# Splitting the first latent projections of a hybrid diffusion step into two halves, the lower one between two pairs of modulation chunks

## What is computed

```python
m_ctx = jnp.split(jax.nn.silu(c_ctx) @ mod_w[l] + mod_b[l], 6, axis=-1)      # shift, scale, gate, ...
m_lat = jnp.split((jax.nn.silu(c) @ mod_w[l] + mod_b[l])[:, None, :], 6, axis=-1)
hp = _modulate(xp, m_ctx[0], m_ctx[1])                                       # x * (1 + scale) + shift
hs = _modulate(xs, m_lat[0], m_lat[1])
q_a, f_f, f_b, i_a, g_a, cq, ckv_raw, kr = jnp.split(h @ w_in, AB_SPLITS, axis=-1)
q = (_rms_norm(cq_raw, q_norm_g) @ w_uq)
kv = (_rms_norm(ckv_raw, kv_norm_g) @ w_ukv)
```

## Time and profile before

| | before |
|---|---|
| median of 3 runs, us | 1290.81 |
| the profiled execution: its own time, us | 1289.75 |
| its span, us | 1287.9 |
| mean granted TensorE clock, share of full | 0.978 |
| PE busy | 1188.9 us (92%) |
| DVE busy | 597.9 us (46%) |
| ACT busy | 352.0 us (27%) |
| instructions | 17510 |
| chain that ended last, by engine | PE 78%, DVE 6%, DMA 6% |
| DMA, mean over the span | 209 GB/s |

### The profile page before, as it was taken

The page is one execution under the profiler, slowest core; times in us unless marked ns, Lnnn a source line. Parts: engine busy times, 40 slices in busy tenths (PEclk is TensorE's granted clock), DMA queues, the critical chain, the costliest instruction groups (busy, mean ns, idle before and its releaser), DMA issues.

```text
span 1287.9 us, 17510 instructions
## 1 busy us (share of the span) xinstructions
PE 1188.9 (92%) x6755; PEld 680.1 (53%) x6755; DVE 597.9 (46%) x1173; ACT 352.0 (27%) x695; POOL 186.9 (15%) x177
## 2 busy tenths in 40 slices
PE   5999999999999989999999877999999998999774
PEld 2554555545546577456555435755555555555441
DVE  2223333310136666768432217079986865332218
ACT  1333444421214543212122125311023111221122
POOL 1000000010000001131323120800000332222210
PEclk9999999999999999998999898999999998999988
DMA  9504476773211204826799969021114438999973
GB/s 348 210 25 177 142 254 239 289 270 114 89 33 40 74 10 163 340 83 232 299 407 409 406 244 393 23 91 66 66 66 171 156 128 316 392 410 408 354 293 150
DMA packets 99666, 269.79 MB, mean 209 GB/s; under 512 B 12811, under 2 KB 15154, under 8 KB 98690
## 3 DMA queue, kind: packets, MB, share of 16 engines
q1 hardware_dynamic: 83632, 234.55, 48.3%
q0 software_dynamic: 15632, 34.02, 7.1%
q10 hardware_dynamic: 322, 0.12, 0.0%
HBM read 257.68 MB, written 31.93 MB: 225 GB/s over the span
## 4 chain that ended last, share of the span: by engine, by line
PE 78%; DVE 6%; DMA 6%; SPq 4%; ACT 3%; issue 2%; ACTq 0%; POOLq 0%; DVEq 0%
PE ps L2285 18%; PE ps L2296 14%; PE ps L2797 8%; PE ps L2814 4%; PE ps L2175 4%; PE ps L2437 3%; DMA ln_rows<-in_moe_w_up 3%; PE ps L2600 3%; PE ps L2785 2%; PE ps L2581 2%; PE ps L2404 2%; PE ps L2746 2%; SPq L710 1%; PE ps L2699 1%; SPq L707 1%
## 5 line engine op out<-in xcount | busy, mean ns | idle before, releaser
L2285 PE MATMUL ps<-h_cm,weights 128*128 128x512 f32 (+1 forms) x832 | 226.8, 434 | 0.0
L2285 PEld LDWEIGHTS ps<-h_cm,weights 128*128 128x128 f32 x832 | 126.3, 191 | 104.0 <-issue 103.7
L2296 PE MATMUL ps<-weights,mix_cm 128*128 128x512 f32 x256 | 112.2, 595 | 0.0
L1769 DVE SCALAR_TENSOR_TENSOR scratch<-scratch,taps_cm 128x655 f32<-128x655 f32 x120 | 101.5, 897 | 2.5 <-ACT scratch L1325 1.0
L2296 PEld LDWEIGHTS ps<-weights,mix_cm 128*128 128x128 f32 x256 | 47.9, 190 | 56.5 <-issue 56.4
L2067 DVE TENSOR_TENSOR scratch<-ps,scratch 128x128 f32<-128x128 f32 x38 | 11.1, 292 | 143.1 <-ACT scratch L1373 143.1
L2296 PE MATMUL ps<-weights,h_cm 128*128 128x512 f32 (+1 forms) x208 | 71.4, 502 | 0.0
L2797 PE MATMUL ps<-weights,scratch 128*64 128x256 f32 x384 | 68.3, 389 | 1.8 <-DMA weights<-in_moe_w_up 1.8
L1442 DVE COPY mod_parts<-ps 128x512 f32<-128x512 f32 x24 | 16.6, 691 | 93.3 <-PE ps L2175 93.3
L1697 DVE SCALAR_TENSOR_TENSOR mix_cm<-mix_cm,gate_rows,ps 128x128 f32<-128x128 f32 x152 | 46.0, 345 | 25.1 <-PE ps L2545 23.0
L2296 PEld LDWEIGHTS ps<-weights,h_cm 128*128 128x128 f32 x208 | 36.3, 190 | 35.6 <-issue 35.6
(11 more groups left out here) (449 smaller groups left out, 2133.1 us busy)
## 6 DMA issues: line engine op xcount, KB each, us to landing
weights<-in_mod_w SPq DMA_DIRECT2D x13, 2048.0 KB, 8.9
x_tm<-in_mod_w SPq DMA_DIRECT2D x10, 2048.0 KB, 8.6
weights<-in_moe_w_gate SPq DMA_DIRECT2D x24, 512.0 KB, 11.6
weights<-in_moe_w_up SPq DMA_DIRECT2D x24, 512.0 KB, 13.4
weights<-in_moe_w_down SPq DMA_DIRECT2D x24, 512.0 KB, 15.7
scratch<-in_moe_w_down SPq DMA_DIRECT2D x21, 512.0 KB, 12.9
weights<-in_ab_w_in SPq DMA_DIRECT2D x5, 2048.0 KB, 12.8
weights<-in_cd_w_in SPq DMA_DIRECT2D x5, 2048.0 KB, 16.0
```

Of the source, the lines that this page charges most:

```text
L1769: ins = V.scalar_tensor_tensor(out=CO[:, j, 0:655], in0=UP[:, j, k:k + 655], scalar=CW[:, 4 * k + j:4 * k + j + 1], in1=CO[:, j, 0:655], o ...
L2285: ins = T.matmul(ps(*name)[:, a:b], w[:, k, col:col + 128], HT[:, k, a:b], start=(k == 0), stop=(k == KD - 1))
L2296: ins = T.matmul(ps(*name)[:, at:at + w.shape[2]], src[:, k, t * 128:t * 128 + 128], w[:, k, :], start=(k == 0), stop=(k == KD - 1))
```

## The change

The lower half of the features (512 of 1024) needs only chunks 0 and 2. The change loads these two first and forms, for all five tiles, the half of the latents that comes from the lower features (groups `ca`), with chunks 1 and 3 and their products in between. ACT puts these partial sums into `CQ`. Afterwards the upper half is formed (groups `cq`), and DVE adds it to `CQ`, which is an added instruction of 672 columns for each tile. The transposes of x are split the same way: `xa` for blocks 0 to 3, `xT` for 4 to 7, each with its slot. The columns of c get a group of their own, `c`, ahead of `vec`. Two times seven short products on the constants are issued whose results nobody reads (`warm_up`). The lower part of the 160 wide weights gets its own place in `mix_cm`. Chunk 3 goes to slot 0, which chunk 0 leaves. GpSimd's four loads of norm vectors and cache wait for the lower latent weights.

```diff
-FIRST_MODS = [("mod", 0), ("mod", 1), ("modb", 0), ("mod", 2), ("modb", 1), ("mod", 3), ("modb", 2), ("modb", 3)]
+FRONT = [("c",), ("mod", 0, 0), ("vec",), ("modb", 0, 0), ("mod", 0, 2), ("modb", 0, 2), ("xa", 0), ("xa", 1), ("ca", 0), ("xa", 2), ("ca", 1),
+         ("xa", 3), ("ca", 2), ("mod", 0, 1), ("modb", 0, 1), ("ca", 3), ("mod", 0, 3), ("modb", 0, 3), ("xa", 4), ("xT", 0, 0), ("ca", 4)]
...
             for t in range(NT):
+                if t + 1 < NT:
+                    g.append(("xT", 0, t + 1))
                 g.append(("cq", t))
...
-        for c in range(4):
-            mod_item(0, c, c)
+        for c, at in ((0, 0), (2, 2), (1, 3), (3, 0)):
+            mod_item(0, c, at)
...
-        proj_item(("cqb",), 2, ("cq", 4), w_in, 3072, AB_IN)
+        cqb_to, cqb_from = slot3(2)[:, 0:8 * (AB_IN - 3072)].rearrange("p (k n) -> p k n", k=8), col_chunk(w_in, 3072, AB_IN)
+        item(("cqb",), 2, ("cq", 4), [(cqb_to[:, 4:8, :], cqb_from[:, 4:8, :])])
+        cqb_low = OTF[:, 4096:4096 + 4 * (AB_IN - 3072)].rearrange("p (k n) -> p k n", k=4)
...
+                    if items[n] == ("mod", 0, 1):
+                        sp.dma_start(X[:, 0:2, :], xs[:, 0:2, :]).then_inc(d_x[0], 16)
+                        sp.wait_ge(d_first, 16)
                         sp.dma_start(cqa_to[:, 0:4, :], cqa_from[:, 0:4, :]).then_inc(d_first, 16)
+                        sp.dma_start(cqb_low, cqb_from[:, 0:4, :]).then_inc(d_first, 16)
+                        sp.dma_start(X[:, 2:4, :], xs[:, 2:4, :]).then_inc(d_x[1], 16)
...
-            pool.wait_ge(d_first, 32)
+            pool.wait_ge(d_first, 48)
...
-            act.wait_ge(d_vec_a, 16 * 11)
+            act.wait_ge(d_c, 32)
             A_(V1[0:16, :], V1[0:16, :], ACT.Silu).then_inc(c_silu, 1)
...
             h_evac0(0)
-            h_evac0(1)
             for t in range(NT):
-                filled(act, "cq", t)
-                release(A_(CQ[:, t, :], ps("cq", t)[:, 0:672], ACT.Copy), "cq", t)
+                if t + 1 < NT:
+                    h_evac0(t + 1)
+                first_half(t)
+            for t in range(NT):
                 emptied(act, "cq", t)
...
             for t in range(NT):
+                if t + 1 < NT:
+                    h_evac0(t + 1)
+                filled(dve, "cq", t)
+                release(V.tensor_tensor(CQ[:, t, :], ps("cq", t)[:, 0:672], CQ[:, t, :], ALU.add), "cq", t)
...
+            def warm_up(at, count):
+
+                for _ in range(count):
+                    T.matmul(at, ident, C[:, 0:128], start=True, stop=True)
...
+                if (l, c) == (0, 0):
+                    warm_up(ps("mod", 0, 0)[:, 512:640], 7)
...
+            def latents(name, t, ks):
+
+                open_group(pe, *name)
+                for at, w in ((0, wa), (512, wb if ks[0] else cqb_low)):
+                    for k in ks:
+                        ins = T.matmul(ps(*name)[:, at:at + w.shape[2]], HT[:, k, t * 128:t * 128 + 128], w[:, k, :],
+                                       start=(k == ks[0]), stop=(k == ks[-1]))
+                close_group(ins, *name)
...
             for t in range(NT):
-                if t:
-                    emptied(pe, "xT", 0, t)
-                    pe.wait_ge(h_half, t + 1)
-                    project_tm(("cq", t), HT, t, [(0, wa), (512, wb)])
-                if t + 2 < NT:
-                    x_turn0(t + 2)
+                if t + 1 < NT:
+                    x_turn0(("xT", 0, t + 1), t + 1)
+                emptied(pe, "xT", 0, t)
+                latents(("cq", t), t, range(4, KD))
                 turn_normed(t - 1 if t else NT)
```

More of the change, by code:

```diff
@@ L160, in psum_groups @@
 def psum_groups():
-    g = [("vec",)]
+    g = list(FRONT)
     for l in range(2):
         if l == 0:
[L165 to L169, removed]
             for t in range(NT):
+                if t + 1 < NT:
+                    g.append(("xT", 0, t + 1))
                 g.append(("cq", t))
-                if t == 0:
-                    g.append(("xT", 0, 1))
-                if t + 2 < NT:
-                    g.append(("xT", 0, t + 2))
                 g.append(("nT", t - 1 if t else NT))
@@ L1485, in _ @@
             steps[0] += 1
+            filled(dve, "c")
+            dve.wait_ge(vec_step, steps[0])
+            release(V.tensor_copy(CT[:, :, 0:2], ps("c")[:, 0:16].rearrange("p (g k) -> p k g", g=2)), "c")
+            mod_row(0, 0)
             filled(dve, "vec")
-            dve.wait_ge(vec_step, steps[0])
-            chain(V.tensor_copy(CT[:, :, 0:2], ps("vec")[:, 192:208].rearrange("p (g k) -> p k g", g=2)))
             chain(V.tensor_copy(MBC[:, :], ps("vec")[:, 208:240]))
@@ L1495, in _ @@
             release(ins, "vec")
+            emptied(dve, "vec")
+            mod_columns(0, 0)
             chain(V.tensor_tensor(LBS[:, 2, :], VC[:, 0:8], VC[:, 8:16], ALU.max))
@@ L1499, in _ @@
             V.tensor_tensor(LBS[:, 1, :], VC[:, 8:16], LBS[:, 2, :], ALU.subtract).then_inc(act_inputs, 1)
+            mod_row(0, 2)
+            mod_columns(0, 2)
             dve.wait_ge(c_silu, 2)
@@ L1511, in _ @@
             chain(ins)
-            for kind, c in FIRST_MODS:
-                drain_mod(kind, 0, c)
+            for c in (1, 3):
+                mod_row(0, c)
+                mod_columns(0, c)
             for c in range(4):
@@ L2189, in side, with x_turn0 @@
                 {"mod": mod_product, "modb": mod_turn}[kind](l, c)
-            def x_turn0(t):
-                pe.wait_ge(d_x[0 if t < 2 else 1], 16 if t < 2 else 32)
-                at_least(pe, h_half, t if t > 1 else 0)
-                open_group(pe, "xT", 0, t)
-                for k in range(KD):
-                    ins = T.transpose(ps("xT", 0, t)[:, k * 128:k * 128 + 128], X[:, t, k * 128:k * 128 + 128], ident)
-                close_group(ins, "xT", 0, t)
+            def x_turn0(name, t):
+                pe.wait_ge(d_x[1 if t in (2, 3) else 0], 32 if t == 4 else 16)
+                open_group(pe, *name)
+                first = 0 if name[0] == "xa" else 4
+                for k in range(4):
+                    ins = T.transpose(ps(*name)[:, k * 128:k * 128 + 128], X[:, t, (first + k) * 128:(first + k) * 128 + 128], ident)
+                close_group(ins, *name)
             def turn_normed(t):
@@ L2255, in early_projection @@
                 if t == 4:
[L2256 removed]
+                    pe.wait_ge(h_half, 1)
                 for k in range(KD):
@@ L2315, in _ @@
             pe.wait_ge(d_first, 16)
+            open_group(pe, "c")
+            warm_up(ps("c")[:, 512:640], 7)
+            pe.wait_ge(c_silu, 1)
+            close_group(T.matmul(ps("c")[:, 0:16], V1[0:16, :], C[0:16, 0:16], start=True, stop=True), "c")
+            emptied(pe, "c")
+            side("mod", 0, 0)
             pe.wait_ge(d_vec, 16 * 6)
-            pe.wait_ge(d_vec_a, 16 * 11)
-            pe.wait_ge(c_silu, 1)
+            pe.wait_ge(d_vec_a, 16 * 9)
+            open_group(pe, "vec")
             v = ps("vec")
@@ L2322, in _ @@
             close_group(T.matmul(v[:, 64:188], V3[:, :], C[0:124, 0:124], start=True, stop=True), "vec")
-            emptied(pe, "vec")
-            for kind, c in FIRST_MODS[:-1]:
-                side(kind, 0, c)
-            x_turn0(0)
-            side(FIRST_MODS[-1][0], 0, FIRST_MODS[-1][1])
             wa, wb = w8(slot3(WITEM[("cqa",)]["slot"])), w8(slot3(WITEM[("cqb",)]["slot"]), AB_IN - 3072)
```

87 lines of the change are left out of this document (37 added, 50 removed).

## The result

| | before | after |
|---|---|---|
| median, us | 1291.41 (20 runs, 1288.19 to 1295.22) | 1294.85 (20 runs, 1288.15 to 1299.22) |
| ratio, 95% interval | | 1.0023 (1.0012 to 1.0034) |
| the profiled execution, us | 1289.75 | 1297.51 |
| its span, us | 1287.9 | 1295.7 |
| mean granted clock | 0.978 | 0.974 |

The changed kernel is 3.0 us slower (1.5 to 4.4 by the interval), less than the 3.9 us that the prediction took for what one measurement tells from no change, but clear over 20 runs. DVE is busy for 4.3 us more, the five additions.

The account below looks back on a forecast made before the run. Small steps under loads bound PE until 33 us, then its own products. 24.0 + 60.7 + 5.7 + 1.7 + 2.4 + 3.6 = 98.1 us against 95.6, 2.5 us later: 1292.3 us from 1289.75; range 1285.5 to 1297.5.

Parts of the forecast that it names:

- within 3.9 us of before and later rather than earlier: Whole kernel: the main forecast, 2.5 us later, within what one measurement tells from no change; chance 0.45.
- The start: Front of the kernel: the first lower latent product starts at 24.0 us instead of 33.1, 9.1 us earlier.
- The slot: Tile 0's transpose `xT`: PE waits 2.4 us for slot 3 while ACT scales tile 4 and copies.
- The copies: Turns of chunks 1 and 3: each waits for the copy of its own product, 0.85 us twice, 1.7 us.
- The moved chunks: Chunks 1 and 3, moved behind the start: product 1.85 and turn 0.98 us each, 5.7 us for both.
- rival C: Between the lower latents: waits absorb the moved chunks, so the kernel is 5.8 us earlier, 1284.0 us; chance 0.13.
- What stays: Latent products of all five tiles: same work, 62.5 us less its slow spell, 60.7 us at full clock.
- The clock: First lower product and tile 4's: the clock falls ahead of each, costing 1.8 us each, 3.6 us together.
- The mark: First matmul with `perm` behind the latents: at 98.1 us against 95.6, 2.5 us later, shifting the end alike.
- a later stage that gains or loses more than the mark: Behind the latents: a sign that the prediction is wrong, as every later stage should shift by the same amount.
- Costs set to nothing: DVE's additions in the norm path (3.7 us, 5.0 for tile 0, under 5.6 us cover) and the warm-up: no cost.
- Rival A: Front: the clock holds, start at 23.1 us, no slow spell, 2.0 us earlier, 1287.8 us; chance 0.15.

Follow-up runs that it names:

- Run 1: Changed kernel with the lower transpose of tile 4 moved ahead of chunk 3; 1290.17 us, ratio 0.9986 to the kernel before.
- Run 2: Run 1's kernel with the products of chunks 1 and 3 one latent product ahead of their turns; 1290.48 us, ratio 0.9981 to the kernel before.
- 4: Changed kernel with the order of Run 2 and the short products of run 3 together; 1287.98 us, ratio 0.9964 to the kernel before.
- run 10: Run 2's order, second warm-up cut to 4 products, 3 more behind chunk 2's product, 5 ahead of the first lower latents; 1288.06 us, ratio 0.9965.
- run 11: Run 2's order with short products in every wait ahead of the first lower latents; 1286.82 us, ratio 0.9964 to the kernel before.
- run 5: Changed kernel with both calls of `warm_up` taken out; 1295.83 us, ratio 1.0031 to the kernel before.
- run 3: Changed kernel with 15 more short, unread products in the waits ahead of the first lower latents; 1292.12 us, ratio 1.0005 to the kernel before.

## Why the prediction was right

It had 1292.3 us, 2.5 us more than its profiled execution; the ratio says 3.0 us. The range held it, and "within 3.9 us of before and later rather than earlier" was what came. The mechanism was right: an earlier start, paid back by moved chunks, two copy waits, a slot wait and the clock. That the size came so near is in part luck, as the points on the clock and on the mark show. Point by point:

- **The start.** Forecast 24.0 us, measured 24.27, 24.38 and 22.86 us in three executions. In the third the start was held by the load, at 22.86 where the sum had 23.1. Two readings of the trace of before were loose. From 17.72 us on PE worked without a gap up to 31.4 us, so no chunk's load held it there; the second profile of before has a wait of 0.79 us for chunk 3, so load and products were nearly level. And the 6.05 us of the first two modulation products were put down to 1.2 GHz from their duration alone, where the profile gives a granted clock of 1.00.
- **The slot.** Forecast 2.4 us of wait for ACT's scaling and copy ahead of tile 0's upper transpose; measured 2.31 us of idle time with ACT L1028 as its end. Run 1 takes it away, together with the slow spell behind it, and wins 4.7 us by the medians.
- **The copies.** Forecast 0.85 us twice; measured 0.88 and 0.81 us. Run 2 takes them away.
- **The moved chunks.** Forecast 5.7 us between products; measured 1.90 + 1.05 us each, 5.9 us. They are what rival C wanted absorbed. Runs 2, 4, 10 and 11 keep them and still have marks ahead of 93 us, as the waits and slow spells were the larger part.
- **What stays.** Forecast 60.7 us; the first profile leaves 100.25 - 24.27 - 5.9 - 1.7 - 2.3 - 4.9 = 61.2 us, 0.5 more.
- **The clock.** Forecast 1.8 us at each of two places. At tile 4 it measured 6.22 - 4.52 = 1.7 us, in three executions out of three. At the first lower latents it was 7.76 - 4.52 = 3.2 us, 3.3 in the second execution, and 2.8 by the 8 wide records of the third (6.41 against 3.60 us): this term was too small by 1.0 to 1.5 us, because I took it from the one slow spell at 33 us, and there the clock was back at 1.00 by 37 us, 4 us after the first product, while here it stayed at 0.50 for 6 us. Worse, the comparison was with a mark of before that itself held 1.7 us of chance: 95.68 us, and 93.94 us the second time.
- **The mark.** Forecast 98.1, measured 100.25, 100.43 and 98.57 us, mean 99.8; before 95.68 and 93.94, mean 94.8. By these five profiles the mark moved by 4.9 us, twice the forecast: the mis-sized terms are the first slow spell and the mark of before, which I took as fixed. The runs moved by 3.0 us (at most 4.4), so the sum came out better than its terms. The five profiles do not show that the rest of the shift is made good later: behind the mark both kernels take the same (1193.6 and 1193.8 us in the mean). But two executions of one kernel differ there by up to 3.5 us, so five profiles are few, and why the runs moved less than the marks stays open. The first profile alone, with 7.8 us at the end for 4.6 at the mark, would have met the prediction's sign of being wrong, "a later stage that gains or loses more than the mark"; the others take that back.
- **Costs set to nothing.** The norm path stayed under its cover. The warm-up was right to be left out of the sum, but in the one profile without it the front is slow throughout (run 5). In the profiles with seven products in the second warm-up and no fillers, a fast one (1.83 us, twice) went with a slow product of chunk 2, and a slow one (3.25 to 3.36 us, four times) with a fast product; why is not shown.

Rival A, the clock that holds, is what run 11 made of the front; in the changed kernel itself it did not appear in three executions.

## What to carry to other kernels

Work pulled forward into a wait for loads pays only what it doesn't push out of that wait: here nine microseconds of earlier start were paid back in two modulation chunks, two copy waits, one slot wait and the clock. In a ring of buffers that is handed out in program order, look at who releases the slot that the next group gets, and whether that engine first does something that only starts now; moving one transpose undid it. Before a slow stretch in one profile is put into a sum, profile the same kernel again.

## What the runs showed that I had not expected

- How fast TensorE goes early in the program is not fixed by the order: with identical code the second warm-up took 1.83, 1.83 and 3.25 us, and the kernel before had its first 8 latent records in 5.25 and in 3.67 us behind the same 0.94 us of idle time.
- The 2.31 us of idle time ahead of tile 0's upper transpose, with only a turn and four transposes between it and chunk 3's product, were followed by slow latents in all five profiles of kernels with that order (the changed kernel three times, runs 3 and 5). In the six profiles without this idle time they took 4.52 us. With products whose results nobody reads, everything from the second warm-up to the first latents ran fast in the one profile of run 11, where no wait in between is longer than 0.54 us.
- Short products cost time where they stand in front of work whose data is there: in run 3 those behind chunk 0's product and its turn (1.60 and 0.69 us) moved chunk 2's product from 16.6 to 18.4 us.
- A busy TensorE is not a fast one: in run 10 it was busy without a break for 12.5 us, and the granted clock was 0.50 all the while.
